# Moving bias, low halves and weighing steps between chunks and attention steps in a two-layer diffusion backbone

## The chip, the cores and the metric

The kernel runs on one core of a Trainium2 chip. The metric is the device time of one execution in microseconds (us); smaller is better. TensorE is PE in the rows (PEld its weight loads), VectorE is DVE, ScalarE is ACT, GpSimd is POOL, SyncE is SP.

## What is computed

One inference step of a two-layer backbone over 128 context tokens and 512 latent tokens of width 1024. A small vector product (`modulation`) gives each layer its shifts, scales and gates; attention and a short convolution run side by side on one input projection of 24 blocks of 128 columns.

```python
def trunk_layer(x, cond, k_ctx, v_ctx, ...):
    shift1, scale1, gate1, shift2, scale2, gate2 = modulation(cond, w_ada_l, b_ada_l)
    h = rms_norm(x, g_mix) * (1 + scale1) + shift1
    mo, k, v = mixer(h, ...)
    x = x + gate1 * mo
    h = rms_norm(x, g_ffn) * (1 + scale2) + shift2
    return x + gate2 * ffn(h), k, v

def mixer(h, ...):
    q, k, v, gb, gc, xin = split(h @ w_in)
    a = softmax(q1 @ k1.T) - lam * softmax(q2 @ k2.T)      # per head, latent queries see 768 keys, context 128
    conv = gb * short_conv(gc * xin, conv_w)
    return concatenate([rms_norm(a @ v), conv]) @ w_out
```

## The kernel before, in words

Every large product is done as three single-precision passes: a weight chunk of 128x1024 is loaded by SP into `raw` (six slots), ACT copies it to `w_hi` (`split_hi`, line 1417), DVE subtracts to get `w_lo` (`split_lo`, line 1997), and PE multiplies at line 800. `w_hi` and `w_lo` have three slots; the splits of chunk c+2 are issued at chunk c. PE writes into four PSUM blocks in turn; `open_block` waits until DVE has emptied the block four items back (`blk_free`).

**First input projection (layer 0).** The order of its items is `IN_SEQ[0]`: k0..k3, q0..q3, v0..v3, gc0..gc3 (each followed by `turn`, in which PE transposes the values at line 989 and DVE copies them at line 2204), xin0..xin3, gb0..gb3. For an item, DVE does in this order: `split_lo` of chunk c+2; `weigh_modulation`, which is the weighing; then it waits for the item's product and takes it (`scaled`, lines 2045 and 2049). For v and gc items ACT then adds the bias (line 1475), and only after it splits the next chunk, on which the next `split_lo` waits. For gb items DVE also runs the convolution (lines 2262 to 2267) before it takes the product.

The weighing computes the modulation of later groups on DVE: a step (group, k) is a 128x1024 piece of `ada_w`, loaded by POOL into one of two buffers (line 1950), times the two conditions, added to an accumulator: two instructions at line 2117 (2115 where k is 0). A group has eight steps, k from 0 to 7. `IN_COUNTS` gives how many steps stand at each item; `mingle` hands out groups 3 and 4 in that order, and after the item that holds k = 7 it puts a `rows` item behind the next item and a `turn` item (line 890) one further. In `rows`, PE waits for all eight steps and sums the accumulator (`sum_conditions`, line 876); PE works in program order, so what is behind waits too. At the last item, gb3, PE first waits until block three back is empty and then issues the first scores of the attention (line 950).

**Attention.** `STEPS` has four small steps (one per head, 128 keys) and then sixteen large ones (768 keys); both layers run the same code. In step i PE computes scores two rows of softmax ahead (`scores`, line 950), transposes the combined weights (`turn_weights`, line 1014) and multiplies the step before with the values (`weigh_values`, line 1007). DVE runs, for i of 2 and more: `combine(i)` (lines 2190 to 2193), `take_output(i - 2)` (line 2294), two `row_max` (line 2176), and then what hangs on i:

```python
if i == 2:
    link(with_bias(gcx[:, CONV_BLOCKS - 1, :], tt[:, 1, :], last_col, cv))
    dve.sem_inc(conv_ready, 1)
if i in CONV_LO:
    j = CONV_LO.index(i)
    lo_part(cc_lo[:, j, :], gcx[:, j, :], cc_hi[:, j, :], operand[l, "cat"] + j + 1)
if i - 4 in HEAD_END:
    sum_head(HEAD_END.index(i - 4))
```

The first is the last convolution block's bias and product with `gb` (line 2054, two instructions), the second the low half of convolution block j (line 2002), the third the sum of squares of a finished head (line 2298), at steps 11, 15 and 19. ACT does the exponentials, copies the transposed weights, and at the steps of `CONV_HI` the high half `cc_hi` (line 1570). The convolution's halves are read by the output projection, which starts in the last step.

## Time and profile before

| | us |
|---|---|
| median of 3 runs | 1841.13 |
| lowest, highest | 1834.24, 1846.46 |
| the profiled execution | 1837.91 |
| its span in the trace | 1836.1 |

The profile is of one execution. "Idle" in square brackets is the time for which the engine did nothing just before the row's instruction, and the arrow names what ended it. PEclk is the granted clock of TensorE as a share of full speed (1.00 is 2.4 GHz, 0.50 is 1.2 GHz). Rows of one engine overlap a little, since an instruction begins before the one ahead has ended; the distance of two starts is what a piece costs. Outside the span lie 1.8 us (1837.91 less 1836.1).

### The profile page before, as it was taken

The numbers are of one execution on the slowest core, as the hardware profiler recorded it, in microseconds if no ns is written. First come the engines' busy times: TensorE is split into PE (matmuls) and PEld (weight loads), VectorE is DVE, ScalarE is ACT, GpSimd is POOL, SyncE is SP. The second block draws the span as 40 slices with busy tenths as digits, with TensorE's granted clock in tenths as the row PEclk, the third lists the DMA queues.
The fourth block names the chain that finished last, engine by engine and source line by source line (L and its number), as shares of the span: only waits on it lengthen the run. The fifth ranks groups of instructions, "written<-read, shape, count | busy, mean of one in ns | idle before, by whom it ended". The sixth has DMA issues, their size and how long they took to land.

```text
span 1836.1 us, 30289 instructions
## 1 busy us (share of the span) xinstructions
PE 1785.5 (97%) x11920; PEld 1664.2 (91%) x11920; DVE 1266.2 (69%) x2047; ACT 789.2 (43%) x1334; POOL 175.2 (10%) x180
## 2 busy tenths in 40 slices
PE   7999999999999999999999999899999999999997
PEld 6999857999999999999999679798989989989885
DVE  2677886567777677545736874576777778778787
ACT  4222265422221222223321564365656656657574
POOL 2000000200001000011000001231000000003211
PEclk8999989999999999999999899899999999999999
DMA  9445200234455444222222001396786878879872
GB/s 364 180 134 169 95 1 1 92 129 148 142 179 174 148 144 144 92 81 81 81 81 81 12 1 24 126 252 214 254 279 226 269 225 267 275 238 349 282 222 69
DMA packets 94707, 290.50 MB, mean 158 GB/s; under 512 B 16232, under 2 KB 24808, under 8 KB 94560
## 3 DMA queue, kind: packets, MB, share of 16 engines
q1 hardware_dynamic: 77280, 233.45, 38.6%
q0 software_dynamic: 17280, 55.05, 9.2%
q8 instruction: 97, 1.59, 0.4%
q14 instruction: 50, 0.41, 0.1%
HBM read 281.98 MB, written 12.28 MB: 160 GB/s over the span
## 4 chain that ended last, share of the span: by engine, by line
PE 79%; DVE 5%; ACT 2%; DMA 1%; issue 1%; POOL 0%; POOLq 0%; DVEq 0%; ACTq 0%; SPq 0%
PE ps L800 41%; PE ps L1179 12%; PE ps L1180 5%; PE ps L1202 5%; PE ps L1212 3%; PE ps L950 3%; PE ps L1007 2%; PE ps L1183 2%; PE ps L1190 2%; DVE w_lo L1997 1%; PE ps L1182 1%; PE ps L1294 1%; DMA raw<-gu_w 1%; PE ps L1014 1%; DVE nbias L2176 1%
## 5 line engine op out<-in xcount | busy, mean ns | idle before, releaser
L1997 DVE TENSOR_TENSOR w_lo<-raw,w_hi 128x1024 fp32r<-128x1024 f32 x394 | 481.7, 1224 | 299.7 <-ACT w_hi L1417 291.5
L1417 ACT ACTIVATE w_hi<-raw 128x1024 fp32r<-128x1024 f32 x394 | 414.1, 1053 | 295.7 <-PE ps L800 182.4
L1179 PE MATMUL ps<-hg,w_hi 128*128 128x320 f32 (+5 forms) x1232 | 345.1, 350 | 0.7 <-DVE w_lo L1997 0.7
L800 PE MATMUL ps<-a_hi,w_hi 128*128 128x320 f32 x1472 | 340.7, 312 | 3.4 <-DVE a_lo L2028 3.4
L800 PE MATMUL ps<-a_hi,w_lo 128*128 128x320 f32 x1472 | 336.6, 310 | 0.0
L800 PE MATMUL ps<-a_lo,w_hi 128*128 128x320 f32 x1472 | 333.9, 308 | 0.0
L1180 PE MATMUL ps<-hg,w_lo 128*128 128x160 f32 (+5 forms) x1232 | 300.0, 244 | 0.0
L800 PEld LDWEIGHTS ps<-a_hi,w_hi 128*128 128x128 f32 x1472 | 247.6, 188 | 8.1 <-issue 3.9
L800 PEld LDWEIGHTS ps<-a_lo,w_hi 128*128 128x128 f32 x1472 | 248.6, 189 | 0.0
L800 PEld LDWEIGHTS ps<-a_hi,w_lo 128*128 128x128 f32 x1472 | 245.3, 188 | 0.0
L1180 PEld LDWEIGHTS ps<-hg,w_lo 128*128 128x128 f32 x1232 | 234.8, 191 | 0.4
L1179 PEld LDWEIGHTS ps<-hg,w_hi 128*128 128x128 f32 x1232 | 232.0, 188 | 2.0 <-DVE w_lo L1997 1.2
L2117 DVE SCALAR_TENSOR_TENSOR ada_raw<-ada_raw,cs 128x1024 f32<-128x1024 f32 x126 | 155.9, 1279 | 1.7 <-DMA ada_raw<-ada_w 0.8
L1202 PE MATMUL ps<-w_hi,ea 128*128 128x512 f32 x308 | 85.0, 398 | 3.6 <-DVE w_lo L1997 3.6
L1950 POOL DMA_DIRECT2D ada_raw<-ada_w x72 | 38.3, 532 | 504.7 <-DVE ada_raw L2117 336.3
L800 PE MATMUL ps<-act_hi,w_hi 128*128 128x320 f32 x352 | 80.6, 310 | 0.0
L800 PE MATMUL ps<-act_hi,w_lo 128*128 128x320 f32 x352 | 80.2, 309 | 0.0
L800 PE MATMUL ps<-act_lo,w_hi 128*128 128x320 f32 x352 | 80.1, 309 | 0.0
L1627 ACT ACTIVATE act_hi<-tt 128x640 fp32r<-128x640 f32 x22 | 16.3, 741 | 137.9 <-DVE tt L2054 137.9
L1202 PEld LDWEIGHTS ps<-w_hi,ea 128*128 128x128 f32 x308 | 57.1, 188 | 17.8 <-DVE w_lo L1997 4.5
L1535 ACT ACTIVATE pr<-ps,nbias 128x768 f32<-128x768 f32 (+1 forms) x80 | 63.5, 795 | 19.3 <-DVE nbias L2176 15.2
L2176 DVE TENSOR_REDUCE nbias<-ps 128x1 f32<-128x768 f32 (+1 forms) x80 | 62.5, 818 | 13.1 <-PE ps L950 12.6
(328 smaller groups left out, 2571.6 us busy)
## 6 DMA issues: line engine op xcount, KB each, us to landing
raw<-gu_w SPq DMA_DIRECT2D x220, 512.0 KB, 4.5
raw<-moe_down_w SPq DMA_DIRECT2D x88, 512.0 KB, 4.4
ada_raw<-ada_w POOLq DMA_DIRECT2D x72, 512.0 KB, 3.8
raw<-in_w SPq DMA_DIRECT2D x48, 512.0 KB, 3.5
raw<-down_w SPq DMA_DIRECT2D x22, 512.0 KB, 3.4
raw<-out_w SPq DMA_DIRECT2D x16, 512.0 KB, 3.4
ada_raw<-ada_w SPq DMA_DIRECT2D x3, 2048.0 KB, 11.0
ada_pro<-ada_w SPq DMA_DIRECT2D x2, 2048.0 KB, 18.8
```

The costliest lines, as they stand in the source:

```text
L800: ins = nc.tensor.matmul(out[:, hf, 0:c1 - c0], w, o[:, c0:c1], start=f, stop=e)
L950: ins = nc.tensor.matmul(score_rows(l, m)[:, c0:c1], qT[rows, h, t * P:(t + 1) * P], kT[rows, h, k0 + c0:k0 + c1], start=True, stop=True)
L1179: nc.tensor.matmul(sums, whi, both, start=(k == 0), stop=False)
L1180: nc.tensor.matmul(out, wlo, rows_[:, k, 0, :], start=False, stop=False)
L1202: ins = nc.tensor.matmul(ps[:, g % 4, hf, :], ea[:, k, LOWER * a:LOWER * a + P], w[:, n % SPLIT, hf * 512:(hf + 1) * 512], start=(k == 0 a ...
L1212: ins = nc.tensor.matmul(ps[:, (g + 1) % 4, hf, :], ea[:, k, P:2 * P], w[:, n % SPLIT, hf * 512:(hf + 1) * 512], start=(k == 0 and w is w_ ...
L1417: nc.scalar.activation(w_hi[:, s, :], raw[:, n % RAW, :], ACT.Copy).then_inc(hi_done, 1)
L1535: nc.scalar.activation(pr[:, i % 2, s, 0:nk], score_rows(l, m)[:, 0:nk], ACT.Exp, bias=nbias[:, m % 4:m % 4 + 1], accum_out=rsum[:, STEPS[ ...
L1950: nc.gpsimd.dma_start(ada_raw[:, m % 2, :], ada_w[grp // 6, KB * (grp % 6) + k])\
L1997: nc.vector.tensor_tensor(w_lo[:, s, :], raw[:, n % RAW, :], w_hi[:, s, :].bitcast(F32), ALU.subtract)\
L2117: ins = nc.vector.scalar_tensor_tensor(ada_acc[:, c, :], part, share, ada_acc[:, c, :], op0=ALU.mult, op1=ALU.add)
L2176: nc.vector.tensor_reduce(nbias[:, m % 4:m % 4 + 1], score_rows(l, m)[:, 0:STEPS[m // 2][3]], AX, ALU.max, negate=True).then_inc(max_done, 1)
```

## The change

Two tables of numbers change; no instruction is added or taken away.

```diff
-IN_COUNTS = {"k": (0, 0, 0, 0), "q": (0, 0, 0, 0), "v": (0, 2, 1, 2), "gc": (1, 1, 1, 1), "xin": (1, 2, 1, 2),
-             "gb": (1, 0, 0, 0), "turn": (0, 0, 0, 0)}
+IN_COUNTS = {"k": (0, 0, 0, 0), "q": (0, 0, 0, 0), "v": (0, 2, 2, 2), "gc": (1, 1, 1, 1), "xin": (2, 2, 1, 1),
+             "gb": (0, 0, 0, 0), "turn": (0, 0, 0, 0)}
...
-CONV_HI, CONV_LO = (0, 1, 3, 4), (2, 3, 4, 5)
+CONV_BIAS, CONV_HI, CONV_LO = 6, (0, 1, 8, 12), (2, 6, 9, 13)
...
-                    if i == 2:
+                    if i == CONV_BIAS:
```

In the first table v2 and xin0 get a second step, xin3 and gb0 lose one. The eighth step of group 3 then stands at gc1 (before at gc2), that of group 4 at xin3 (before at gb0), and both `rows` and both `turn` items come one chunk earlier.

The first place is DVE in the first input projection, items v2 and v3 (`w_lo` is a split, `ada_raw` the weighing, `vT` the values taken). Before:

```order
L1997 TENSOR_TENSOR w_lo<-raw,w_hi 128x1024
L2117 SCALAR_TENSOR_TENSOR ada_raw<-ada_raw,cs 128x1024 x2
L2045 TENSOR_REDUCE bcol<-ps 128x2
L2049 TENSOR_TENSOR vT<-ps,ss 128x640
L1997 TENSOR_TENSOR w_lo<-raw,w_hi 128x1024
L2117 SCALAR_TENSOR_TENSOR ada_raw<-ada_raw,cs 128x1024 x4
L2045 TENSOR_REDUCE bcol<-ps 128x2
L2049 TENSOR_TENSOR vT<-ps,ss 128x640
```

DVE at the same two items now:

```order
L1997 TENSOR_TENSOR w_lo<-raw,w_hi 128x1024
L2117 SCALAR_TENSOR_TENSOR ada_raw<-ada_raw,cs 128x1024 x4
L2045 TENSOR_REDUCE bcol<-ps 128x2
L2049 TENSOR_TENSOR vT<-ps,ss 128x640
L1997 TENSOR_TENSOR w_lo<-raw,w_hi 128x1024
L2117 SCALAR_TENSOR_TENSOR ada_raw<-ada_raw,cs 128x1024 x4
L2045 TENSOR_REDUCE bcol<-ps 128x2
L2049 TENSOR_TENSOR vT<-ps,ss 128x640
```

Two more instructions of the weighing stand at v2, ahead of the taking of its product.

The second place is PE behind the second transposing of values (line 989, after gc1). Before, the products of gc2 follow it:

```order
L989 MATMUL ps<-idn,vT 128x128 x5
L800 MATMUL ps<-a_hi,w_hi 128x320
L800 MATMUL ps<-a_hi,w_hi 128x324
L800 MATMUL ps<-a_lo,w_hi 128x320 x2
L800 MATMUL ps<-a_hi,w_lo 128x320
```

On PE at that place now (`pick` marks the sum of the eight weighing steps):

```order
L989 MATMUL ps<-idn,vT 128x128 x5
L876 MATMUL ps<-ada_raw,pick 2x256 x8
L800 MATMUL ps<-a_hi,w_hi 128x320
L800 MATMUL ps<-a_hi,w_hi 128x324
L800 MATMUL ps<-a_lo,w_hi 128x320 x2
```

The sum at line 876 moved one chunk ahead and now stands before the products of gc2.

The third place is DVE in the attention, steps 2 and 3 (`gcx<-tt,bcol` is the convolution's bias, `cc_lo` a low half, `nbias` a row maximum, `pr` the combining). Before:

```order
L2176 TENSOR_REDUCE nbias<-ps 128x1 x2
L2054 SCALAR_TENSOR_TENSOR gcx<-tt,bcol 128x128
L2054 SCALAR_TENSOR_TENSOR gcx<-tt,bcol 128x512
L2002 TENSOR_TENSOR cc_lo<-gcx,cc_hi 128x640
L2190 RECIPROCAL rinv<-rsum 128x1
L2191 SCALAR_TENSOR_TENSOR cmix<-rinv,nlam,rsum 128x1
L2193 SCALAR_TENSOR_TENSOR pr<-pr,cmix 128x128
L2294 COPY ada_raw<-ps 128x128
L2176 TENSOR_REDUCE nbias<-ps 128x1 x2
L2002 TENSOR_TENSOR cc_lo<-gcx,cc_hi 128x640
```

DVE in step 6 and the start of step 7 now:

```order
L2294 COPY ada_raw<-ps 128x128
L2176 TENSOR_REDUCE nbias<-ps 128x1 x2
L2054 SCALAR_TENSOR_TENSOR gcx<-tt,bcol 128x128
L2054 SCALAR_TENSOR_TENSOR gcx<-tt,bcol 128x512
L2002 TENSOR_TENSOR cc_lo<-gcx,cc_hi 128x640
L2190 RECIPROCAL rinv<-rsum 128x1
L2191 SCALAR_TENSOR_TENSOR cmix<-rinv,nlam,rsum 128x1
```

The bias and one low half moved from small steps to one large step; of the other low halves one stays at step 2, and two stand at steps 9 and 13 (before at 4 and 5). The high halves of blocks 2 and 3 move on ACT from steps 3 and 4 to 8 and 12. The order on POOL and SP is the same as before.

## Rows read from the trace of the kernel before

**Rows 1.** The page, busy time: us, share of the span, instructions
```profile
PE 1785.5 (97%) x11920; PEld 1664.2 (91%) x11920; DVE 1266.2 (69%) x2047; ACT 789.2 (43%) x1334; POOL 175.2 (10%) x180
```

**Rows 2.** Windows, layer 0: length, busy PE, PEld, DVE, ACT, POOL, PEclk, DMA
```profile
118.00:155.15 37.15, 37.15 (x258) 36.88 (x256) 28.54 (x34) 9.83 (x15) 3.72 (x7) 1.00 0.54 173
...
215.85:217.26 1.41, 0.00 (x0) 0.03 (x1) 1.23 (x4) 1.30 (x3) 0.00 (x0) 1.00 0.13 52
```

**Rows 3.** Timeline of PE, first input projection: start, length, line, tiles, [idle]
```profile
146.86 0.71 PE L989 MATMUL ps<-idn,vT 128*128 128x128 f32 x5
...
154.44 0.71 PE L989 MATMUL ps<-idn,vT 128*128 128x128 f32 x5
155.83 1.05 PE L876 MATMUL ps<-ada_raw,pick 128*2 128x256 f32 x16 [0.68 <-DVE ada_raw L2117]
```

**Rows 4.** Timeline of DVE, the same stretch, same columns
```profile
130.12 1.23 DVE L1997 TENSOR_TENSOR w_lo<-raw,w_hi 128x1024 fp32r<-128x1024 f32 x1 [2.03 <-ACT w_hi L1417]
...
139.16 1.22 DVE L1997 TENSOR_TENSOR w_lo<-raw,w_hi 128x1024 fp32r<-128x1024 f32 x1 [2.03 <-ACT w_hi L1417]
...
145.61 1.23 DVE L1997 TENSOR_TENSOR w_lo<-raw,w_hi 128x1024 fp32r<-128x1024 f32 x1 [1.00 <-ACT w_hi L1417]
...
153.20 2.48 DVE L2117 SCALAR_TENSOR_TENSOR ada_raw<-ada_raw,cs 128x1024 f32<-128x1024 f32 x2
```

**Rows 5.** Transfers that POOL issues at line 1950, 100 to 240 us
```profile
DMA to landing us min/median/max: 3.7/3.8/5.8
```

**Rows 6.** Timeline of PE at the last chunk of the first input projection
```profile
217.26 0.49 PE L950 MATMUL ps<-kT,qT 64*128 64x128 f32 x4 [1.42 <-DVEq L2277]
```

**Rows 7.** Windows at full and at half granted clock, columns as in rows 2
```profile
40.00:44.00 4.00, 3.15 (x12) 3.15 (x13) 4.00 (x9) 4.00 (x9) 0.00 (x0) 0.50 1.06 380
48.00:52.00 4.00, 4.00 (x30) 4.00 (x29) 1.54 (x2) 0.00 (x0) 0.00 (x0) 1.00 0.02 7
225.60:244.42 18.82, 14.38 (x58) 7.42 (x57) 15.39 (x37) 10.28 (x29) 0.00 (x0) 0.73 0.00 0
1015.29:1037.60 22.31, 18.59 (x75) 10.65 (x75) 17.88 (x41) 12.14 (x34) 0.00 (x0) 0.69 0.01 1
1173.20:1184.00 10.80, 7.63 (x43) 7.38 (x42) 6.82 (x35) 1.31 (x3) 2.04 (x2) 0.68 0.43 152
1185.16:1196.00 10.84, 7.65 (x50) 7.67 (x51) 7.73 (x17) 7.34 (x10) 6.01 (x6) 0.84 0.83 246
```

**Rows 8.** Timeline of PE in the routing stage of layer 1
```profile
1176.11 1.90 PE L1285 MATMUL ps<-tok,sel 128*128 128x2 f32 x10 [2.91 <-DVE sel L2475]
...
1188.35 2.30 PE L1294 MATMUL ps<-idn,gx 128*128 128x128 f32 x16 [3.19 <-DMA gx<-h_rows,slot_row]
```

**Rows 9.** Timeline of PE in the attention of layer 0 and of layer 1
```profile
244.42 0.85 PE L1014 MATMUL ps<-idn,pr 128*128 128x128 f32 x6 [0.59 <-DVE ada_raw L2294]
...
266.93 1.56 PE L950 MATMUL ps<-kT,qT 64*128 64x512 f32 x8
...
270.93 1.56 PE L950 MATMUL ps<-kT,qT 64*128 64x512 f32 x8
...
275.27 1.56 PE L950 MATMUL ps<-kT,qT 64*128 64x512 f32 x8
...
1027.71 1.98 PE L950 MATMUL ps<-kT,qT 64*128 64x512 f32 x8 [1.41 <-ACT pr L1535]
```

**Rows 10.** Timeline of DVE in the attention of layer 0
```profile
232.21 1.00 DVE L2054 SCALAR_TENSOR_TENSOR gcx<-tt,bcol 128x128 f32<-128x128 f32 x2
233.36 0.83 DVE L2002 TENSOR_TENSOR cc_lo<-gcx,cc_hi 128x640 fp32r<-128x640 f32 x1
234.10 0.16 DVE L2190 RECIPROCAL rinv<-rsum 128x1 f32<-128x1 f32 x1
...
240.14 1.82 DVE L2176 TENSOR_REDUCE nbias<-ps 128x1 f32<-128x768 f32 x2 [0.98 <-PE ps L950]
```
## The prediction

> **What bounds the kernel now.** I read the page first. PE is busy 97% of the span and DVE 69% [rows 1]: almost all time is PE's own work, and an edit counts only where PE stands still, or where it runs at half clock. So the second view was the list of PE's waits, and the third the windows of the two stages that the change touches. In the first input projection PE has no hole from 118 to 155.15 us [rows 2]. Then come two: 0.68 us before the `rows` sum of group 3, ended by the weighing on DVE [rows 3], and 1.42 us before the first scores, at gb3 [rows 6]; in that one DVE is busy 1.23 of 1.41 us [rows 2], so DVE is behind there. In the attention a large step takes 4.00 us (270.93 less 266.93) and PE has hardly a gap [rows 9]. Only in the steps around the turn from small to large does PE wait for the softmax: 1.41 us in layer 1, 0.59 us in layer 0 [rows 9].
>
> The fourth view was the granted clock. It is 0.73 on average over 18.82 us at the start of layer 0's attention and 0.69 over 22.31 us in layer 1 [rows 7]. Since the clock has two levels, 1.00 and 0.50, these are 2 x 0.27 x 18.82 = 10.2 us and 2 x 0.31 x 22.31 = 13.8 us at 1.2 GHz. What that costs is in the products: 3.15 us for 12 of them at 0.50 (0.2625 each), 4.00 us for 30 at 1.00 (0.133 each) [rows 7]; a microsecond at half clock loses 0.49 us of product work.
>
> **Part 1, the weighing.** No work is added; only its place changes. From one split to the next DVE needs 9.04 us at an item with two steps (130.12 to 139.16) and 6.45 us at one with a single step (139.16 to 145.61) [rows 4]. The chain is closed: the split waits for ACT (2.03 us idle ahead of it), ACT for DVE's taking of the product. So the second step at v2 puts everything behind it on DVE back by 9.04 - 6.45 = 2.59 us. On the other hand the eighth step is one item earlier, 6.45 us. Before, it ended at 153.20 + 2.48 = 155.68 and the sum began at 155.83 [rows 3, 4]. Now it can end at 155.68 - 6.45 + 2.59 = 151.82, and the sum begins at 151.97.
>
> PE, however, comes to the sum a whole chunk earlier, after the second transposing: 146.86 + 0.71 = 147.57 [rows 3]. Its wait is therefore 151.97 - 147.57 = 4.40 us, where it was 0.68. Behind the waiting sum stand the products of gc2, whose weights are ready, and all that follows; nothing is ahead that could fill the hole. The transfers don't end later than this: by the chain above each step begins about 6 us after its POOL transfer is issued, and those land in 3.7 to 5.8 us [rows 5]. SP's loads shift by at most the same 2.59 us with six slots ahead; I put that at nothing.
>
> The 1.42 us at gb3 [rows 6] go: gb0 no longer carries a weighing step, the blocks that the first scores need are those of `turn` and gb1 instead of gb2, and PE arrives later by the hole. Next late there is DVE's combining of step 0, which ends about when gb3's product does, so nothing takes its place.
>
> The hole also has a price in clock. Holes of 2.91 and 3.19 us in layer 1 [rows 8] lie in windows with a mean clock of 0.68 and 0.84 [rows 7], that is 6.9 and 3.5 us at 1.2 GHz. 4.40 us is longer than both. Part of the low time may lie in the hole itself, so I take 4.4 us of the mean of 5.2: 4.4 x 0.49 = 2.2 us. The bounds are 0 and 10.2 x 0.49 = 5.0 us, the longest single spell of the attention.
>
> Sum of part 1: -0.68 + 4.40 - 1.42 + 2.2 = +4.5 us.
>
> **Part 2, the attention, twice.** What is taken out of the small steps: the bias costs DVE 233.36 - 232.21 = 1.15 us and a low half 234.10 - 233.36 = 0.74 us [rows 10]. That looks like a lot, but behind them DVE waits for PE: the row maxima of step 4 begin after 0.98 us of idle time, ended by PE [rows 10], since the scores at half clock take longer than DVE's extras. So in steps 2 to 4 the extras cover a wait, and their removal gives nothing. At step 5 of layer 0 PE waited 0.59 us for DVE [rows 9]; without the low half of step 4 that goes but for what the exponential then holds, and I take 0.5 us. Layer 1 at that place is slower by the clock, so 0. If no row maximum waited for PE, 1.15 + 2 x 0.74 = 2.6 us a layer would be gained; 0 and 2.6 are the bounds.
>
> What is put into the large steps: the trace shows one extra of this size there. The sum of squares of a head (line 2298) is an instruction over the same 640 columns as a low half; the step with it runs from 270.93 to 275.27, 4.34 us instead of 4.00 [rows 9]. So 0.74 us of DVE work costs 0.34, and 0.40 is DVE's slack in a step. Steps 9 and 13 cost 0.34 each. Step 6 gets bias and low half together, 1.15 + 0.74 = 1.89 us, less 0.40 of slack: 1.49 us. A layer pays 1.49 + 0.34 + 0.34 = 2.17 us; bounds 0 (all hidden) and 1.89 + 1.48 = 3.4 us (no slack). The two high halves on ACT, which is busy 43% of the span [rows 1], I count at nothing; uncovered they would be at most about 0.7 us each, taking the low half's length for them.
>
> Sum of part 2 without the clock: 2 x 2.17 - 0.5 = +3.8 us.
>
> The 1.49 us at step 6 are a hole in PE before the transposing of step 7, and here the rows disagree on the clock. A hole of 1.41 us in layer 1 [rows 9] lies in a stretch with 13.8 us at half clock; one of 1.42 us at gb3 lies in a stretch at 1.00 [rows 2, 6]. I take an even chance in each layer, so most likely one of the two falls: a spell of 5.2 us (mean of 6.9 and 3.5) x 0.49 = 2.5 us.
>
> By the Trainium skill, "TensorE: Matmul & The Clock Gate", section "HAM oscillation — how this bites in real kernels", the clock is lost to long waits between bursts of matmuls; a hole as short as step 7's would not count. By that rule the 2.5 us fall away; the fall in layer 1 around the 1.41 us hole speaks against it, the full clock after gb3's hole for it.
>
> **The sum.** 4.5 + 3.8 + 2.5 = +10.8 us on the profiled execution's 1837.9 (span 1836.1 and 1.8 around it), so 1848.7, rounded to 1849. That execution is 3.2 us below the median of the three runs, which themselves spread over 12.2 us; against the median the sum is +0.4%. One per cent, about what a measurement of this kernel can tell from no change, is 18.4 us.
>
> **Rivals.**
> - *Short holes leave the clock alone.* All as above without the 2.5 us: 1846. For it the gb3 hole, against it layer 1's.
> - *Both layers lose the clock at step 7*: 2.5 us more, 1851. For it that PE's matmuls in the attention are small and many.
> - *A long low spell after the `rows` hole*, the 10.2 us kind, and xin0 and xin1 with two steps each (9.04 us against about 7 of PE) holding PE too: +2.8 and up to 4 us, 1856. Against it: PE then lags, which gives DVE room.
> - *The other side: the small steps keep the full clock.* If taking DVE's extras out of steps 2 to 5 closes the holes there, the 10.2 and 13.8 us at half clock go: 24.0 x 0.49 = 11.8 us. With no fall at step 7 the time is 1837.9 + 8.3 - 11.8 = 1834, faster than before by a little. It decides from the point at which the windows of 225 to 244 us read 1.00. Against it: in layer 0 the first row maximum for a large step already waits for half-clock scores, and the first moved instruction comes after it, at 232.21 [rows 10]; only the 1.41 us hole of layer 1 lies behind moved work, and it is ended by the exponential of a row that PE delivers late.
> - *The change does nothing that shows*: the weighing is ready when PE comes, and the steps hide all: about -2, 1836. Against it the closed chain of rows 4.
>
> **Chances.** Forecast 0.40; short holes 0.22; both layers 0.20; long spell 0.07; small steps at full clock 0.06; nothing 0.05. The range 1839 to 1858 leaves out the two last and half of the long spell. Slower by over 1% (above 1859.5) needs the long spell or a run to run shift on top of the forecast: 0.10. Faster by over 1% needs more than the best rival gives: 0.02. Within 1%: 0.88.
>
> **What would show it.** In the changed profile: a wait of about 4.4 us before line 876 near 152 us, ended by line 2117, and PEclk below 1.00 just after; no wait before the first line 950; the end of the input projection some 4 us later. In the attention: starts of line 950 some 5.5 us apart around step 7, and 4.34 us apart at steps 9 and 13; the waits of 0.98 us on DVE at step 4 longer. I am wrong if line 876 waits under 2 us, if the step 7 hole is missing, or if the windows at the start of the attention read 1.00.

## The result, and the profile after

| kernel | median us | lowest to highest | runs |
|---|---|---|---|
| before | 1838.43 | 1834.24 to 1846.46 | 20 |
| after | 1844.99 | 1837.35 to 1851.69 | 20 |

The ratio is 1.0033, with a 95% interval of 1.0023 to 1.0043: the changed kernel is slower by 6.1 us (4.2 to 7.9). Here and below a difference in us is the ratio taken times the time of before; the medians alone can lie a little apart from it (here 6.6 us). That is within one per cent, the likeliest case of the prediction, and in its range, but the sum was +10.8 us. The median of before was 1841.13 us over the three runs shown ahead of the prediction and is 1838.43 us over these 20; the comparison uses these. The profiled execution of after took 1846.57 us with a span of 1844.8 us, 8.7 us more than the span of before: it is one of the longer ones, and its rows have to be read with that in mind.

The page of the changed kernel, busy time, and from its forty slices the line of the granted clock (each figure is tenths of full speed in one slice of 46 us):

```profile
PE 1788.1 (97%) x11920; PEld 1665.3 (90%) x11920; DVE 1266.5 (69%) x2047; ACT 788.6 (43%) x1334; POOL 176.8 (10%) x180
...
PEclk8999989999999999999999899999999999999999
```

Beside [rows 1] the counts of instructions are the same on every engine, and DVE's busy time differs by 0.3 us: nothing was added. PE is busy 2.6 us longer with the same matmuls, so some of them ran at a lower clock; the other 6.1 us of the 8.7 are idle time. The sixth slice (231 to 277 us) and the twenty-third (1015 to 1061 us), both 8 and not 9, hold the starts of the two attentions. The same line of before has one 8 more, in the twenty-sixth slice (1148 to 1193 us, the routing stage of layer 1).

**The weighing.** PE's timeline at the sum of group 3 and at the first scores of layer 0 (start, length, engine, line, tiles, then in brackets the idle time before it and what ended it):

```profile
147.14 0.71 PE L989 MATMUL ps<-idn,vT 128*128 128x128 f32 x5
152.23 1.89 PE L876 MATMUL ps<-ada_raw,pick 128*2 128x256 f32 x16 [4.39 <-DVE ada_raw L2117]
...
221.27 0.49 PE L950 MATMUL ps<-kT,qT 64*128 64x128 f32 x4
```

Against [rows 3] the sum now stands behind the second transposing and no longer behind the third, and it waits 4.39 us instead of 0.68. Against [rows 6] the first scores have no idle time before them. The DVE rows of the same stretch show why the sum waits:

```profile
142.02 1.23 DVE L1997 TENSOR_TENSOR w_lo<-raw,w_hi 128x1024 fp32r<-128x1024 f32 x1 [2.03 <-ACT w_hi L1417]
...
148.47 1.22 DVE L1997 TENSOR_TENSOR w_lo<-raw,w_hi 128x1024 fp32r<-128x1024 f32 x1 [0.99 <-ACT w_hi L1417]
149.62 2.47 DVE L2117 SCALAR_TENSOR_TENSOR ada_raw<-ada_raw,cs 128x1024 f32<-128x1024 f32 x2
```

One item still takes 6.45 us (142.02 to 148.47), as in [rows 4], and the last weighing ends at 149.62 + 2.47 = 152.09; the sum starts 0.14 us later. The windows show what it did to the clock (start and end of the window, length, busy time of PE, PEld, DVE, ACT and POOL, then PEclk, the granted clock as a share of full speed, the DMA share and GB/s):

```profile
148.00:160.00 12.00, 7.77 (x53) 6.38 (x54) 8.28 (x11) 2.51 (x4) 1.05 (x2) 0.86 0.51 169
```

12 us at a mean of 0.86 are 2 x 0.14 x 12 = 3.4 us at 1.2 GHz. The same window of before reads 1.00:

```profile
148.00:160.00 12.00, 11.32 (x89) 10.45 (x88) 10.14 (x16) 3.93 (x6) 1.06 (x2) 1.00 0.50 173
```

In after the clock fell inside the hole. The last microsecond of it that is wholly idle reads

```profile
151.00:152.00 1.00, 0.00 (x0) 0.00 (x0) 1.00 (x1) 0.00 (x0) 0.00 (x0) 0.95 0.80 283
```

so the fall came at 151.9 us, 0.3 us before the sum started and after PE had stood still for some 4 us.

**The attention.** Windows of 20 us from near its start, in layer 0 and in layer 1, same columns:

```profile
230.00:250.00 20.00, 16.61 (x65) 9.21 (x64) 14.18 (x33) 9.76 (x29) 0.00 (x0) 0.66 0.00 1
250.00:270.00 20.00, 18.14 (x122) 12.49 (x120) 17.67 (x33) 13.97 (x31) 0.00 (x0) 1.00 0.00 1
1022.00:1042.00 20.00, 16.63 (x64) 9.32 (x65) 14.17 (x33) 9.85 (x29) 0.00 (x0) 0.66 0.00 1
1042.00:1062.00 20.00, 18.07 (x121) 12.39 (x119) 17.67 (x33) 13.91 (x31) 0.00 (x0) 1.00 0.01 1
```

And PE's timeline in layer 0, steps 7 to 10, where the row at 258.00 is the transposing of step 7 and that at 270.35 the transposing of step 10:

```profile
254.96 1.56 PE L950 MATMUL ps<-kT,qT 64*128 64x512 f32 x8
258.00 0.85 PE L1014 MATMUL ps<-idn,pr 128*128 128x128 f32 x6 [1.48 <-DVE ada_raw L2294]
...
260.48 1.56 PE L950 MATMUL ps<-kT,qT 64*128 64x512 f32 x8
...
268.47 1.56 PE L950 MATMUL ps<-kT,qT 64*128 64x512 f32 x8
270.35 0.85 PE L1014 MATMUL ps<-idn,pr 128*128 128x128 f32 x6 [0.32 <-DVE ada_raw L2294]
...
272.83 1.56 PE L950 MATMUL ps<-kT,qT 64*128 64x512 f32 x8
```

The step with the bias and a low half takes 260.48 - 254.96 = 5.52 us instead of 4.00, with a hole of 1.48 us in it; one with a low half alone takes 272.83 - 268.47 = 4.36. The 1.48 us hole lies at 256.5 to 258.0, inside the window 250 to 270, and that window reads 1.00. In layer 1 it is the same. The half clock lies where it lay before [rows 7], at the small steps, and is 2 x 0.34 x 20 = 13.6 us long in either layer. There DVE still waits for PE's scores, longer than the 0.98 us of [rows 10], as its row maxima of step 4 say:

```profile
244.38 1.82 DVE L2176 TENSOR_REDUCE nbias<-ps 128x1 f32<-128x768 f32 x2 [1.37 <-PE ps L950]
```

Where the 8.7 us of the two spans went, from the starts of the same instructions in both traces: 0.3 us ahead of the second transposing (147.14 less 146.86, before the change is reached); 74.13 instead of 70.40 us from there to the first scores of layer 0, +3.7; the attention of layer 0, first scores to last, 80.60 instead of 78.35, +2.2; that of layer 1 80.60 instead of 79.36, +1.2; all else +1.2.

### The profile page after: what moved, and what is told of

The parts are those of the page before. It is cut to its first block, busy times and chain, and to the rows that moved or that the text cites. A ratio compares the mean times of both kernels' runs of the same rounds, so it can differ in the third digit from the quotient of the medians.

```text
span 1844.8 us, 30289 instructions
## 1 busy us (share of the span) xinstructions
PE 1788.1 (97%) x11920; PEld 1665.3 (90%) x11920; DVE 1266.5 (69%) x2047; ACT 788.6 (43%) x1334; POOL 176.8 (10%) x180
## 4 chain that ended last, share of the span: by engine, by line
PE 85%; DVE 6%; DMA 3%; ACT 2%; issue 2%; POOL 1%; SPq 0%; POOLq 0%; DVEq 0%; ACTq 0%
PE ps L800 49%; PE ps L1179 10%; PE ps L1202 6%; PE ps L1180 4%; PE ps L1212 4%; PE ps L950 2%; PE ps L1007 2%; PE ps L1190 2%; DMA raw<-gu_w 2%; PE ps L1183 1%; DVE nbias L2176 1%; DVE w_lo L1997 1%; PE ps L1182 1%; PE ps L866 1%; DMA yab<-y_rows,late 1%
```

## The experiments

Twelve sets of runs (11 is the kernel of 3 once more), in three groups: 1 to 4, 5 to 8 and 9 to 12, each group on a chip of its own, with the kernel before beside it. The 95% intervals of the ratios are about 2 us wide to either side. "Ratio" is the time over that of before. The stretches of half clock in the attention differ from run to run, in the kernel before too, so a profile alone does not decide a few microseconds. Two lengths are read from each profile: **the front**, from the second transposing of the first input projection to the first scores (70.40 us before, 74.13 after), and **the layer**, from the first scores to the last of one layer's attention.

The record also has the mean granted clock of every run of these groups and of after. From it comes the time at half clock in the whole execution, 2 x (1 - clock) x span. On average over the runs of a kernel it is:

| kernel | us at half clock | kernel | us at half clock |
|---|---|---|---|
| before (104 runs) | 49 | 6 | 32 |
| after | 53 | 7 | 33 |
| 1 | 41 | 8 | 46 |
| 2 | 51 | 9 | 39 |
| 3 | 44 | 10 | 28 |
| 4 | 47 | 11 | 46 |
| 5 | 48 | 12 | 44 |

These means are good to 1 us for before and 1 to 3 us for the others. Within the 104 runs of before the time goes up by 0.29 us with each microsecond at half clock (correlation 0.76), so a difference of 8 us in this table goes with some 2.3 us of time.

**1. The attention's part alone.** The tables of the convolution as in after, the weighing's counts as in before:

```diff
-CONV_HI, CONV_LO = (0, 1, 3, 4), (2, 3, 4, 5)
+CONV_BIAS, CONV_HI, CONV_LO = 6, (0, 1, 8, 12), (2, 6, 9, 13)
...
-                    if i == 2:
+                    if i == CONV_BIAS:
```

> Only the attention table and the bias's step are the changed ones; the weighing is as before. Theory (the extras come out from under waits for PE and cost what is over DVE's 0.4 us of slack in a large step): +3.5 to +4 us against before; a hole of 1.5 us before line 1014 of step 7 in both layers, steps of 4.34 us at 9 and 13, no gain in steps 2 to 4. Rival (the price is the weighing's alone, the attention is even): 0 to +1 us.

1838.63 us, ratio 1.0003 [0.9992, 1.0015]: +0.5 us (-1.5 to +2.8). The forecast's +3.5 to +4 lies outside. The costly step is there all the same; here is the hole in layer 1:

```profile
1042.85 0.84 PE L1014 MATMUL ps<-idn,pr 128*128 128x128 f32 x6 [1.48 <-DVE ada_raw L2294]
```

No half clock follows it in either layer. Something gives back nearly all that the large steps pay, and the record points at what: these 12 runs had 8 us less at half clock than before, which goes with 2.3 us of time. Whether the new table brings that about or chance does is open, since the other pairs don't repeat it (after 53 beside 51 in 2; 8 with 46 beside 44 and 46 in 3 and 11).

Two layers can be set side by side that differ in the table alone. In layer 0 of 1 and in layer 0 of before the half clock is 10.2 us long and starts 12.7 us behind the first scores. The scores of steps 5 and 6, of 1 and then of before:

```profile
241.50 1.56 PE L950 MATMUL ps<-kT,qT 64*128 64x512 f32 x8 [0.73 <-ACT pr L1535]
...
245.69 1.56 PE L950 MATMUL ps<-kT,qT 64*128 64x512 f32 x8
```

```profile
242.27 1.56 PE L950 MATMUL ps<-kT,qT 64*128 64x512 f32 x8 [0.68 <-ACT pr L1535]
...
246.89 1.56 PE L950 MATMUL ps<-kT,qT 64*128 64x512 f32 x8
```

With the first scores at 216.44 and 217.26, the scores of step 5 come after 25.06 us in 1 and 25.01 in before: taking DVE's extras out of steps 2 to 4 gave nothing at this clock. Step 5 then takes 4.19 us instead of 4.62, a gain of 0.4 us, and the layer 80.14 instead of 78.35, 1.8 us more.

**2. The weighing's part alone.**

```diff
-IN_COUNTS = {"k": (0, 0, 0, 0), "q": (0, 0, 0, 0), "v": (0, 2, 1, 2), "gc": (1, 1, 1, 1), "xin": (1, 2, 1, 2),
-             "gb": (1, 0, 0, 0), "turn": (0, 0, 0, 0)}
+IN_COUNTS = {"k": (0, 0, 0, 0), "q": (0, 0, 0, 0), "v": (0, 2, 2, 2), "gc": (1, 1, 1, 1), "xin": (2, 2, 1, 1),
+             "gb": (0, 0, 0, 0), "turn": (0, 0, 0, 0)}
```

> Only the weighing's table is the changed one; the attention is as before. Theory (PE comes to the sum of group 3 a chunk too early): +3.5 to +4.5 us against before, with a wait of about 4.4 us before the first line 876, one spell at half clock after it, and no wait of 1.4 us before the first scores. Rival (the weighing part is even, since the wait at the end goes): 0 to +1 us.

1841.73 us, ratio 1.0023 [1.0011, 1.0035]: +4.2 us (2.0 to 6.4), as expected. The hole is the same; the clock after it, by the window in the same place as above, was low for 2 x 0.28 x 12 = 6.7 us, twice as long as in after:

```profile
150.39 1.89 PE L876 MATMUL ps<-ada_raw,pick 128*2 128x256 f32 x16 [4.39 <-DVE ada_raw L2117]
```

```profile
149.00:150.00 1.00, 0.00 (x0) 0.00 (x0) 1.00 (x2) 0.00 (x0) 0.00 (x0) 0.50 0.87 229
148.00:160.00 12.00, 9.61 (x58) 8.23 (x59) 6.91 (x10) 2.07 (x3) 1.05 (x2) 0.72 0.56 174
```

The first window lies inside the hole: here 1.4 us of the half clock passed before the sum started at 150.39, while PE had nothing to do. The front is 220.50 - 145.29 = 75.21 us. This kernel has the attention as before, and in this execution layer 0 kept the full clock throughout. PE's timeline there shows what half clock usually hides:

```profile
237.92 0.30 PE L1014 MATMUL ps<-idn,pr 128*128 128x128 f32 x1 [1.98 <-DVE ada_raw L2294]
...
239.86 1.56 PE L950 MATMUL ps<-kT,qT 64*128 64x512 f32 x8 [1.42 <-ACT pr L1535]
241.96 0.85 PE L1014 MATMUL ps<-idn,pr 128*128 128x128 f32 x6 [0.54 <-DVE ada_raw L2294]
```

At full clock PE waits for DVE in the small steps, 1.98 us at step 3, so the extras that the change takes out of these steps are worth something there. The layer took 76.70 us.

**3. The sum one chunk later.** The weighing's steps as in after, but the sum of group 3 back where it was, behind the third transposing, and the attention as before:

```diff
-                spots = [j for j in range(i + 1, len(items)) if allowed(j)]
+                spots = [j for j in range(i + 1 + (2 if g == 3 else 0), len(items)) if allowed(j)]
```

> The weighing's changed table with the attention of before, but the sum of group 3 and its turn stand one chunk later, where they stood before. Theory: the hole of 4.4 us is a matter of the sum's place, not of the steps' places; so no wait before line 876, no spell at half clock there, no wait before the first scores: -2 us against before. Rival (DVE's backlog from the second step at v2, xin0 and xin1 is what costs): +1 us or more, and PE waits elsewhere in the projection.

1833.93 us, ratio 0.9976 [0.9965, 0.9987]: 4.4 us faster than before. PE does not wait for the sum, the window 147 to 155 us is full and at 1.00, and the first scores do not wait either:

```profile
154.24 0.71 PE L989 MATMUL ps<-idn,vT 128*128 128x128 f32 x5
154.87 1.04 PE L876 MATMUL ps<-ada_raw,pick 128*2 128x256 f32 x16
```

```profile
147.00:155.00 8.00, 8.00 (x61) 7.80 (x63) 5.87 (x8) 2.92 (x5) 0.53 (x1) 1.00 0.57 188
```

The front is 214.93 - 146.65 = 68.28 us, 2.1 less than before, as the two waits of 0.68 and 1.42 us say. The 4.4 us were more than the expected 2; run again (11 below) it came to 2.0. The runs had 5 us less at half clock than before, which goes with 1.5 us of it. So the moved steps cost nothing where PE comes to their sum at the old place. What costs is where the sum stands, which follows by rule from the place of the eighth step.

**4. The bias left at step 2**, the rest of the attention's part as in 1:

```diff
-CONV_BIAS, CONV_HI, CONV_LO = 6, (0, 1, 8, 12), (2, 6, 9, 13)
+CONV_BIAS, CONV_HI, CONV_LO = 2, (0, 1, 8, 12), (2, 6, 9, 13)
```

> The weighing as before; the attention as changed, but the last convolution block's bias stays at step 2 (low halves at 2, 6, 9, 13). Theory (DVE's work in step 2 is hidden behind scores that PE makes at half clock): 2 x 1.15 = 2.3 us less than the attention part alone, about +1.5 us against before, and the row maximum of step 3 starts no later. Rival (work at step 2 costs what it takes): the same time as the attention part alone, +3.5 to +4 us.

1838.66 us, ratio 1.0004 [0.9994, 1.0014]: +0.7 us (-1.1 to +2.6), by the times the same as in 1. The interval holds the theory's +1.5 and not the rival's +3.5 to +4, but not the 2.3 us less than 1 either. The runs of 4 had 6 us more at half clock than those of 1, so the two times don't compare one table with the other. The traces do. DVE's step 6 now has only a low half, and the step of PE that waits for it takes 4.36 us instead of 5.51, in both layers. What the bias costs at step 2 depends on the clock:

- Layer 1 of 4 and layer 1 of 8 (below; the whole new table) both have one spell of 6.8 us at half clock, starting 11.7 and 11.9 us behind the first scores. The scores of step 6 come after 28.63 us (1037.35 - 1008.72) and 28.62 us (1034.55 - 1005.93): here the bias at step 2 cost nothing. The layer takes 78.36 us instead of 79.51.
- Layer 0 of 4 and layer 1 of 1 both have two spells of 3.4 us, with full clock between them. The scores of step 6 come after 28.81 us (247.73 - 218.92) and 27.87 us (1035.81 - 1007.94): here it cost 0.94 of its 1.15 us.

So the forecast's view that the bias at step 2 lies wholly under a wait is right for a long spell at half clock and wrong without one.

**5. The hole filled with idle matmuls.** The weighing as in 2, and 32 single-precision matmuls of the ones tile ahead of the sum; nothing reads their results, nor those of such matmuls in 6, 7, 9 and 10.

```diff
             def sum_conditions(grp, g):
 
+                if grp == 3:
+                    keep_busy(g, 32)
                 pe.wait_ge(ada_done, KB * (grp - 2))
```

> The weighing's table alone as changed (attention of before), and 32 idle matmuls of 128x128 ahead of the wait at line 876, whose results nobody reads; they take some 4 us of the 4.4 us hole. The hole stays as long, only the clock is kept. Theory (the hole costs its length and a spell at half clock): no spell near 150 us in the trace, 1.6 to 3.3 us less than the weighing part alone, +1 to +2.5 us against before. Rival (the spell lies mostly in the hole or is hidden): the same time as the weighing part alone, +4 us.

1844.12 us, ratio 1.0033 [1.0022, 1.0045], +6.1 us: outside the +1 to +2.5 expected, because the filling was too long.

```profile
148.78 7.31 PE L885 MATMUL ps<-ones 128*128 128x128 f32 x64
156.02 1.05 PE L878 MATMUL ps<-ada_raw,pick 128*2 128x256 f32 x16
```

One idle matmul took 7.31 / 32 = 0.228 us (the trace has two records for each), so the sum began 7.8 us behind the start of the transposing, where it is 5.1 in 2: 2.7 us later than it need have. The clock stayed full, but this run does not price it.

**6 and 7. The small steps filled, with the old and with the new table of the convolution.** Both have the weighing of 3. In the small steps PE runs idle matmuls where it would wait for the softmax: 4, 1, 6, 2 ahead of the transposing of steps 0, 1, 3, 4 and 4, 1, 8, 2 ahead of the scores of steps 1, 2, 4, 5. In 6 the convolution's parts stand as before, in 7 as after.

```diff
+                def hold(out, count):
+                    for _ in range(count):
+                        nc.tensor.matmul(out, ones[:], ones[:], start=True, stop=True)
...
                 for i, (h, t, k0, nk) in enumerate(STEPS):
+                    if i in (1, 2, 4, 5):
+                        pe.wait_ge(exp_done, 2 * l * NS + 2 * i + 1)
+                        hold(score_rows(l, 2 * i + 3)[:, 0:P], {1: 4, 2: 1, 4: 8, 5: 2}[i])
                     scores(2 * i + 3, 2 * i + 4)
...
-                    pe.wait_ge(comb_done, l * NS + i + 1)
                     if i > 0:
                         pe.wait_ge(pt_ready, l * NS + i)
+                    if i in (0, 1, 3, 4):
+                        hold(turned_weights(l)[:, 0:P], {0: 4, 1: 1, 3: 6, 4: 2}[i])
+                    pe.wait_ge(comb_done, l * NS + i + 1)
```

> The sum one chunk later, with the attention table of before, and idle matmuls of 128x128 in the holes of attention steps 0 to 5 (4, 1, 6, 2 ahead of the transposing of steps 0, 1, 3, 4; 4, 1, 8, 2 ahead of the scores of steps 1, 2, 4, 5), into PSUM that PE owns then. Theory (the half-clock spells of 7 to 14 us a layer start with these holes and cost 1 to 2.7 us a layer): no spell at the start of the attention, its length from first to last scores about 76.7 us in both layers, 3 us less than the later sum alone. Rival (the matmuls take as long as they save): spells gone and the same time.

> As the filled steps with the old table, but with the changed attention table. At full clock PE waits for DVE's extras in steps 3 to 5 (1.98, 0.54, 0.57 us in a layer without a spell), so here the removal must gain. Theory (gain at full clock about 2.6 us a layer against 2.17 us of price in steps 6, 9 and 13): within 1 us of the old table, perhaps 0.8 us faster. Rival (nothing is gained in the small steps at any clock): 3.8 to 4.3 us slower than the filled steps with the old table.

6: 1836.69 us, ratio 0.9994 [0.9983, 1.0006]. 7: 1839.02 us, ratio 0.9999 [0.9987, 1.0011]. In neither does the attention of either layer fall below 1.00, and so these two traces compare the tables at full clock. PE's scores of steps 3 and 6 in 6:

```profile
231.03 1.56 PE L950 MATMUL ps<-kT,qT 64*128 64x512 f32 x8
...
245.16 1.56 PE L950 MATMUL ps<-kT,qT 64*128 64x512 f32 x8
```

and of 7:

```profile
229.27 1.56 PE L950 MATMUL ps<-kT,qT 64*128 64x512 f32 x8
...
242.53 1.56 PE L950 MATMUL ps<-kT,qT 64*128 64x512 f32 x8
```

From the scores of step 3 to those of step 6 kernel 6 needs 14.13 us and 7 needs 13.26. With 0.05 in the step behind them the small steps gain 0.92 us. That is the least they gain: in 7 PE has no wait left in this stretch, the idle matmuls fill it, so a further gain can't show. In the large steps 7 pays 1.52 for the bias and the low half and 0.35 for each further low half, 2.22. The layer took 77.77 us in 6 and 79.09 in 7, both layers alike within 0.01: the new table costs 1.3 us a layer at full clock, or less. By the medians of the runs the two layers together are 2.3 us, or 0.9 us by the ratios. For 7, the theory said within 1 us and the rival 3.8 us or more; the traces have 2.6. For 6, the spells went as expected but not the time: it is 3.3 us slower against before than 3 and 0.9 slower than 11, where it was to be 3 us faster. The filling was too long and took away what it gained (from the scores of step 0 to those of step 1 PE takes 3.20 us instead of 2.07).

**8. The sum one chunk later and the new table of the convolution**, the diffs of 3 and 1 together.

> The sum one chunk later with the changed attention table, that is the changed kernel with its sum put back. Theory (the two parts add up; the attention part alone measured +0.5 us, the later sum -4.4 us): about -4 us against before and 10 us less than the changed kernel. Rival (the attention part costs 2.7 us, as stages of equal low time show): -1.5 to -2 us against before.

1837.64 us, ratio 0.9992 [0.9980, 1.0003], 1.5 us faster than before, which is the rival's figure; the theory's -4 lies outside. The kernel of 3 was 4.4 and on repetition 2.0 faster, so by these figures the new table cost 3 or 0.5 us, each give or take 3 us, and 3 and 11 ran in other groups. Holes of 1.48 us again in both layers; the windows 250 to 270 and 1040 to 1060 us read 1.00 here as well.

**9. The hole filled to its length**: as 5, with fewer idle matmuls.

```diff
-                    keep_busy(g, 32)
+                    keep_busy(g, 17)
```

> The weighing's table alone as changed, with 17 idle matmuls instead of 32 ahead of the wait at line 876: a matmul of this kind took 0.228 us of PE in the run with 32 (7.31 us), so these take about 3.9 us and end before the wait does. Theory (the hole costs its 4.4 us and a spell at half clock of 3.4 to 6.8 us, 1.7 to 3.3 us of products): no spell at 150 us, sum at line 876 at 152 us as in the changed kernel, about +2 us against before. Rival (the clock price is nil, since DVE and not PE sets the pace after the hole): +4 us as the weighing part alone.

1837.62 us, ratio 0.9999 [0.9985, 1.0012]: -0.2 us (-2.8 to +2.2), not the rival's +4.

```profile
146.49 0.71 PE L991 MATMUL ps<-idn,vT 128*128 128x128 f32 x5
147.03 3.96 PE L885 MATMUL ps<-ones 128*128 128x128 f32 x34
151.49 1.04 PE L878 MATMUL ps<-ada_raw,pick 128*2 128x256 f32 x16 [0.50 <-DVE ada_raw L2119]
```

```profile
148.00:160.00 12.00, 11.50 (x96) 10.65 (x96) 8.31 (x13) 1.97 (x3) 1.06 (x2) 1.00 0.54 173
```

The sum waits just as long as in 2, for the same weighing, but the clock stays full, and the front is 219.12 - 146.49 = 72.63 us. That is 2.2 more than before: the delay by itself, which by the waits is 4.40 - 0.68 - 1.42 = 2.3. The same front with 3.4 us of half clock was 1.5 us longer (after) and with 6.7 us it was 2.6 longer (2). By the medians of their runs 9 is 4.1 us faster than 2, more than the trace of the front holds, and against before the 2.2 us are at the very end of the interval. The runs of 9 had 12 us less at half clock than those of 2 (39 and 51), and only the 6.8 us behind the hole are explained; the rest lies elsewhere in the program. So the price of the clock behind the hole is taken from the traces of the front.

**10, 11 and 12.** 10 is 6 with fewer idle matmuls:

```diff
-                    if i in (1, 2, 4, 5):
+                    if i in (1, 4, 5):
...
-                        hold(score_rows(l, 2 * i + 3)[:, 0:P], {1: 4, 2: 1, 4: 8, 5: 2}[i])
+                        hold(score_rows(l, 2 * i + 3)[:, 0:P], {1: 2, 4: 5, 5: 1}[i])
...
-                    if i in (0, 1, 3, 4):
-                        hold(turned_weights(l)[:, 0:P], {0: 4, 1: 1, 3: 6, 4: 2}[i])
+                    if i in (0, 3, 4):
+                        hold(turned_weights(l)[:, 0:P], {0: 2, 3: 6, 4: 1}[i])
```

11 is 3 once more, on the same chip as 10 and 12. 12 leaves the sum where it was in another way, with steps of the weighing taken from gb0 but not past it:

```diff
-IN_COUNTS = {"k": (0, 0, 0, 0), "q": (0, 0, 0, 0), "v": (0, 2, 1, 2), "gc": (1, 1, 1, 1), "xin": (1, 2, 1, 2),
-             "gb": (1, 0, 0, 0), "turn": (0, 0, 0, 0)}
+IN_COUNTS = {"k": (0, 0, 0, 0), "q": (0, 0, 0, 0), "v": (0, 2, 1, 2), "gc": (1, 1, 1, 1), "xin": (2, 2, 2, 1),
+             "gb": (0, 0, 0, 0), "turn": (0, 0, 0, 0)}
```

> The later sum with the attention table of before and fewer idle matmuls in the attention: 2, 6, 1 ahead of the transposing of steps 0, 3, 4 and 2, 5, 1 ahead of the scores of steps 1, 4, 5. The first version kept the clock but was 1.1 us too long at step 0 and 0.3 us at step 3. Theory: no spell, 76.7 us from first to last scores in both layers, 1 to 2 us less than the later sum without them on the same chip. Rival (the spells start all the same with so few): stages of 78 us and the same time.

> The later sum once more, the same kernel as before: its trace explains 2.1 us (two waits gone), its runs gave 4.4 us. Theory (2.1 us is right, the rest was chance): -2 us against before, interval around it. Rival (something outside the projection is faster too): -4 us again.

> The weighing's steps for v and gc items as before (group 3 ends at gc2), xin items 2, 2, 2, 1 and none at gb0 (attention of before). Theory: the 0.68 us wait before the first line 876 stays, the 1.4 us wait before the first scores goes: -1.4 us against before. Rival (DVE, with three items of two steps in a row, falls behind and PE waits in the xin or gb items): 0 or slower.

10: 1833.55 us, ratio 0.9977 [0.9966, 0.9987], 4.2 us faster than before. 11: 1835.37 us, ratio 0.9989 [0.9977, 1.0001], 2.0 us faster. 12: 1834.42 us, ratio 0.9981 [0.9969, 0.9994], 3.5 us faster. 10 is 2.2 us under 11 by the ratios, 1 to 2 us were expected. 11 gives the theory's -2, with the rival's -4 just inside its interval (-4.2 to +0.2). 12 was to gain 1.4 us, which its interval holds; it had 6 us less at half clock than before. The windows at the start of the attention, of 10 in layer 0 and then of 11 in layer 0 and in layer 1:

```profile
220.00:240.00 20.00, 17.53 (x111) 12.52 (x110) 17.74 (x44) 10.81 (x32) 0.00 (x0) 1.00 0.05 20
```

```profile
220.00:240.00 20.00, 13.09 (x76) 8.04 (x75) 17.85 (x45) 11.31 (x33) 0.00 (x0) 1.00 0.00 1
1006.00:1026.00 20.00, 16.46 (x71) 10.52 (x72) 15.84 (x41) 9.23 (x29) 0.00 (x0) 0.74 0.09 27
```

The same instructions in 11 kept the full clock in layer 0 and lost it in layer 1. With the idle matmuls both layers keep it, and the layer takes 76.86 and 76.85 us, against 76.70 and 78.84 in 11. The front is 68.27 us in 11 and 69.02 in 12, where the 0.68 us before the sum stay and the 1.42 us before the first scores go:

```profile
155.00 1.04 PE L876 MATMUL ps<-ada_raw,pick 128*2 128x256 f32 x16 [0.68 <-DVE ada_raw L2117]
```

Kernel 10 beats both kernels of this case: 4.2 us under before and, as after is 6.1 us over it, about 10 under after.

## Why the prediction was right or wrong

**The direction and the first part: right, by the reasons given.** The hole was to be 4.40 us with the sum at 151.97; it is 4.39 us with the sum at 152.23, and the trace of after runs 0.28 us late even ahead of the change. The wait before the first scores is gone, and nothing took its place. Alone this part costs 4.2 us (2.0 to 6.4), where the sum had 4.5. The runs 3 and 11 show that the hole comes from the sum's place: with the same steps and a later sum the hole is gone and the time is below before. Kernel 12 shows that the gain at the first scores was to be had without it.

**Its clock term: right in kind, somewhat too big.** 2.2 us were taken for 4.4 us at half clock. In after the spell was 3.4 us long and the front 1.5 us longer than the same front at full clock in 9. In 2 it was 6.8 us (by narrower windows than above), for 2.6 us. The bounds of 0 and 5.0 held. The prediction had said that part of the low time may lie in the hole itself, and so it does: 0.3 us in after and 1.4 us in 2. For the rest a microsecond of half clock cost 1.5 / 3.1 = 0.48 and 2.6 / 5.4 = 0.48 us, the 0.49 of the sum.

**The price in the large steps: right.** 1.49 at step 6 and 0.34 at steps 9 and 13 were forecast; the traces of 6 and 7 have 1.52, 0.35 and 0.35. One instruction of the same size in a step like these was enough to say how much slack DVE had there.

**The step that failed is the clock's fall at step 7**, the 2.5 us in "I take an even chance in each layer, so most likely one of the two falls". Holes of 1.47 or 1.48 us at step 7 were there in after and in 1, 7 and 8, in two layers each: eight, and not one was followed by half clock. The rival *Short holes leave the clock alone* was right. The evidence that misled was the 1.41 us hole of layer 1 in [rows 9], which lies in a stretch that is at half clock for the most part. The windows of before ahead of that hole, around it (1026.3 to 1027.7) and behind it:

```profile
1018.60:1025.20 6.60, 6.42 (x18) 2.99 (x17) 4.25 (x12) 2.77 (x10) 0.00 (x0) 0.50 0.00 1
1025.40:1028.60 3.20, 1.49 (x9) 0.92 (x9) 3.13 (x8) 2.08 (x6) 0.00 (x0) 1.00 0.00 0
1028.80:1035.40 6.60, 6.30 (x25) 3.64 (x22) 5.41 (x10) 3.08 (x8) 0.00 (x0) 0.50 0.00 1
```

There are two spells. The first had begun 8 us ahead of the hole; the hole itself is at full clock, and 1 us behind it the second spell starts. So a fall did follow this hole, but it stands in the small steps, where PE waits every few microseconds (it is busy for 1.49 of the 3.20 us), and the hole at step 7 stands between full steps. The prediction took the one as evidence for the other. The rule of the Trainium skill that the prediction weighed ("TensorE: Matmul & The Clock Gate", section "HAM oscillation — how this bites in real kernels") says that long waits between bursts of matmuls lose the clock. With it the sum would have been 8.3 us, and at the holes of step 7 the rule and the traces agree.

**The other step that failed, by less: "their removal gives nothing" in the small steps.** Taken was 0.5 us for layer 0 and 0 for layer 1, because DVE waits there for scores at half clock. Where PE is at half clock that is right to 0.1 us: layer 0 of 1 against layer 0 of before gains nothing up to step 5 and 0.4 us at it. At full clock the gain is 0.92 us a layer or more (6 against 7). And whether PE is at half clock there differs between the executions of one kernel, and even between the layers of one: layer 0 of 2 had none, and there PE waits for DVE. The profile of before was one draw, and a term that depends on the clock was taken from it as if it always held.

**How the sum stands now.** The waits, +2.3, and the clock behind the hole, +1.5, make 3.8 us for the first part. The attention costs 2 x 1.3 = 2.6 us with both layers at full clock and 2 x 1.8 = 3.6 us with both as layer 0 of before and of 1 had it. Together that is 6.4 to 7.4 us, beside 6.1 (4.2 to 7.9) measured. The attention's share rests on two pairs of traces; by the runs alone it is not well known: +0.5 us (-1.5 to +2.8) in 1, which with the 2.3 us that go with its lower half clock would be 2.8; 1.9 us as the difference of after and 2 by their ratios; 0.5 or 3 from 8. The forecast's range had room for a sum without the 2.5 us of step 7, so the number came out inside it although that step failed.

**The profiled executions.** Of the 8.7 us between the two spans 3.5 lie in the attention, where the two profiles also differ in half clock: 10.2 us in layer 0 of before, 13.6 in layer 0 of after, and about 13.6 in layer 1 of both. In the routing stage of layer 1 it is the other way, 13.6 us in before and 6.8 in after. Where the 1.2 us in the rest of the program lie was not followed up.

## What to carry to other kernels

An item that sums up the steps of another engine belongs to a place where those steps are done when PE arrives, and PE must have work ahead of it. When a planner ties the sum to the last step, moving that step earlier moves the sum earlier as well, and by a whole chunk of PE's work where the step itself gained only a part of one. Before a hole is charged with a fall of the clock, look in narrow windows at where each spell starts and at what else PE did around the hole; a hole among many others says little about an equal one in dense work. A term that depends on the clock wants several executions: where the clock differs from run to run, compare the two versions in stretches whose half clock has the same length and place, or with that stretch held at full clock. The mean granted clock of each run says whether two sets of runs had the same share of half clock at all.

## What the runs showed of the hardware that was not expected

**Half clock comes in portions, and not in every execution.** In all these traces the half clock in the attention and behind the sum adds up to about 3.4, 6.8, 10.2 or 13.6 us, or to none. The same instructions gave a different length from one execution to the next. With the table of before and no idle matmuls, a layer without any took 76.70 us (2, 9, 11; 5 in layer 1), one with 6.8 us took 77.76 to 78.01 (2, 9, 12), one with 10.2 us 78.20 to 78.84 (before, 3, 5, 11, 12) and one with 13.6 us 79.36 to 79.38 (before, 3). So 2.7 us a layer, 5.4 over both, hang on this alone, beside a spread of 12.2 us in the 20 runs of before. Kernel 10, whose profile has none there, spread over 5.6 us in 12 runs, and kernel 11 over 8.6. By the granted clock of the runs, 10 was at half clock for 28 us on average and 11 for 46.

**Its price depends on what PE does meanwhile.** Behind the hole of the sum, among dense products, a microsecond at half clock cost 0.48 us. At the start of the attention 6.8 us cost 1.1 to 1.3 us and 13.6 us cost 2.7, so 0.16 to 0.20 us for each, since PE waits for other engines there much of the time, and waits less where its own work takes longer (at step 3 1.98 us in layer 0 of 2, 0.26 in layer 0 of before). The prediction's rival *small steps keep the full clock* took 0.49 for it, 11.8 us for 24.0; by these layers it would be 4 to 5.

**The length of a hole is not all that counts.** A single hole of 1.47 or 1.48 us between full steps never cost the clock in eight cases. At the small steps it is otherwise: shorter holes, several in a row, were followed by a fall in most layers. PE's timeline of after, where the clock fell:

```profile
230.69 0.33 PE L1014 MATMUL ps<-idn,pr 128*128 128x128 f32 x1 [0.62 <-DVEq L2277]
231.65 0.49 PE L950 MATMUL ps<-kT,qT 64*128 64x128 f32 x4 [0.63 <-ACT pr L1535]
232.40 0.33 PE L1014 MATMUL ps<-idn,pr 128*128 128x128 f32 x1 [0.26 <-DVE pr L2193]
...
233.18 2.35 PE L950 MATMUL ps<-kT,qT 64*128 64x128 f32 x6 [0.23 <-ACT pr L1535]
```

and of 2 at the same instructions, where it did not:

```profile
229.92 0.33 PE L1014 MATMUL ps<-idn,pr 128*128 128x128 f32 x1 [0.62 <-DVEq L2277]
230.88 0.49 PE L950 MATMUL ps<-kT,qT 64*128 64x128 f32 x4 [0.63 <-ACT pr L1535]
...
232.41 1.56 PE L950 MATMUL ps<-kT,qT 64*128 64x128 f32 x6 [0.23 <-ACT pr L1535]
```

The holes are alike, 0.62, 0.63, 0.26 and 0.23 us among small matmuls, and then the same scores take 2.35 us in the one and 1.56 in the other. Of the 22 layers without idle matmuls (before, after, 1 to 5, 8, 9, 11, 12) 18 lost the clock at the start of the attention, for 6.8 to 13.6 us in all. In 15 it fell 10.9 to 13.1 us behind the first scores, which is among these four small holes or within 1.2 us of them. In the other three (2 and 9 in layer 1, 12 in layer 0) it came through them and fell behind the next, the 1.98 us hole of step 3 or the 1.42 us one that follows it; four layers came through those too. The six layers with idle matmuls (6, 7, 10) kept the clock. What decides between two executions of the same code was not found. In the 4.4 us hole of the sum the clock fell both times (after, 2), after some 4 and 3 us of standing still, and not when idle matmuls stood in it (5, 9).

**Filling has a price of its own.** One idle matmul of 128 x 128 in single precision took 0.228 us at full clock, so 17 of them fill 3.9 us of the 4.4 us hole. With 32 (5) the front took 75.41 us, as long as with the bare hole in 2 (75.21), and in the attention the difference between too many (6) and nearly enough (10) was 0.9 us a layer.
